# Splitting the operands of a projection into high and low parts, and moving one slab of products into the norms ahead of it

## The chip, the cores and the metric

The kernel runs on one NeuronCore of a Trainium2 chip, in one launch. The metric is device microseconds of an execution: the median of several runs, and beside it one profiled execution, from which every row below comes. The engines are TensorE (PE in rows; PEld its weight loads), VectorE (DVE), ScalarE (ACT), GpSimd (POOL) and the DMA queues, which SyncE (SP) and GpSimd issue. TensorE writes to eight banks of PSUM of 512 fp32 columns each. Its clock has two levels in this trace: 1.0 (2.4 GHz) and 0.50 (1.2 GHz) in the column of the granted clock.

## The reference, cut to what matters

Two transformer blocks follow each other over x of [1024 tokens, 1024]. All arithmetic is fp32. The change touches the end of the first block's mixers and the seam between the two blocks:

```
y  = concatenate([y_a, y_b, y_c, y_d], axis=-1) @ w_out          # [1024, 1024] @ [1024, 1024]
x1 = layer_norm(ALPHA * x + g1 * y, ln1_w, ln1_b)
h  = x1 * (1 + sc2) + sh2
x2 = layer_norm(ALPHA * x1 + g2 * swiglu(h, w_ffn_in, w_ffn_out), ln2_w, ln2_b)
...
h3   = rms_norm(x2, norm_mix_2)
proj = h3 @ w_in_2      # r_q, r_k, r_v, r_g, d_q, d_c, d_pe, d_g, i_q, i_k, i_w
```

The 440 columns d_c, d_pe, i_q, i_k and i_w of `proj` are the first slab of the projections; the others follow in slabs of 512 columns.

## The kernel before, in words

The program is a chain of stages, each a block of its own: all five engines run their own hand-written list of instructions, tied by semaphores, and a stage begins when every engine has ended the last one. Tokens are cut into eight tiles of 128; `i` or `n` names a tile, `k` one of eight groups of 128 features.

**Mixers** (`stage_mixers`, block at L894). In its end VectorE normalises the first mixer's heads in two halves (L1396 to L1406), asking ScalarE for a square root in each (L1204), TensorE transposes them (L1135) and ScalarE drains them into `yT` (L1207). After the last attention product SyncE loads `w_out` in four transfers of two k (L919).

**Join** (`stage_join`, L1409). For each tile TensorE makes `y @ w_out` in fp32 (L1458): two halves of 512 columns, eight k each, every product two instructions. VectorE multiplies by g1 out of PSUM (L1501), adds ALPHA x (L1505), norms (L1522 to L1528), applies sc2 and sh2 (L1510, L1511) into one of two buffers `jn_h`. GpSimd stores x1 (L1437). After the matmuls of tile i TensorE transposes `jn_h` of tile i - 1 (L1448) into banks 4 to 7, ScalarE drains it as the high part (L1470: a copy that rounds to fp32r) and VectorE subtracts it to get the low part (L1489). The two pairs of banks 0, 1 and 2, 3 take the products of even and odd tiles.

**Feed-forward** (`stage_ffn`). All products are made of high and low parts (`product`, L1538): high x high, high x low and low x high, three fp32r matmuls for one product. It takes the tokens in two halves h, and begins with tiles 0 to 3. Per unit of 24 matmuls ScalarE makes the high part of a weight tile (L1643), VectorE the low part (L1729). The hidden layer is a loop of eleven iterations of four units, of which the first stands alone.

**End of the first block** (`stage_first_end`, L1810). Tiles 4 to 7 are transposed back (`back`, L1852), normed on VectorE (`norm`, with L1934 first), scaled on ScalarE by a row sum (`size`, `inverse`, `scale`), weighed on GpSimd (L1835) and, like tiles 0 to 3, transposed (`turn`, L1863), drained by ScalarE (`take`, L1883) and VectorE (`low`, L1947).

**Projections** (`stage_project`). Weights come by k (L2040, four buffers), ScalarE and GpSimd split them (L2133, L2226), and slab 0 runs with k outside and the eight tiles inside, into eight banks. While it runs VectorE makes the angles of the rotary embedding, after positions, frequencies and a gain have been loaded behind the first four weights.

Of the kernel before, what the change touches and what calls it, by code (L numbers as in the profile page):

```python
# [120 lines left out]
def setup(nc, I, out):  # L121
# [23 lines left out]
    K.yT = [at(f"yT{k}", 24 + 4 * k, [P, T]) for k in range(6)] + [K.ydT[:, k, :] for k in range(2)]  # L145
# [667 lines left out]
def stage_mixers(K):  # L813
# [17 lines left out]
    K.wo_in = K.sem("mx_woin")  # L831
# [62 lines left out]
    with nc.Block() as block:  # L894
        @block.sync
        def _(sp):
# [21 lines left out]
            for k in range(0, KT, 2):  # L918
                sp.dma_start(K.wo[:, k:k + 2, :], wo[:, k:k + 2, :]).then_inc(K.wo_in, 16)  # L919
# [220 lines left out]
        def _(act):  # L1140
# [268 lines left out]
def stage_join(K):  # L1409
# [6 lines left out]
    h = [K.at(f"jn_h{s}", 48 + 4 * s, [P, D]) for s in range(2)]  # L1416
# [4 lines left out]
    mm, mev, sq, x1r, hr, tr, thi, tev, chain = (K.sem("jn_" + n) for n in "mm mev sq x1r hr tr thi tev chain".split())  # L1421
    stored = [K.sem(f"jn_st{s}") for s in range(2)]
    with nc.Block() as block:
# [18 lines left out]
        def _(pe):  # L1442
            def turn(i):
# [3 lines left out]
                for k in range(KT):  # L1447
                    last = nc.tensor.transpose(K.bank[4 + 2 * (i % 2) + k // 4][:, (k % 4) * P:(k % 4 + 1) * P],  # L1448
                                               h[i % 2][:, k * P:(k + 1) * P], K.ident[:])
                last.then_inc(tr, 1)  # L1450

            pe.wait_ge(K.wo_in, 16 * KT // 2)
            for i in range(NT):
                if i >= 2:
                    pe.wait_ge(mev, i - 1)
                for b in range(2):
                    for k in range(KT):
                        last = nc.tensor.matmul(K.bank[2 * (i % 2) + b][:], K.yT[k][:, i * P:(i + 1) * P], wo[:, k, b * HALF:(b + 1) * HALF],  # L1458
                                                start=(k == 0), stop=(k == KT - 1))
                last.then_inc(mm, 1)  # L1460
                if i:
                    turn(i - 1)
            turn(NT - 1)

        @block.scalar
        def _(act):
# [5 lines left out]

            for i in range(NT):
                act.wait_ge(sq, 2 * i + 1)
                nc.scalar.activation(rs, rs, ACT.Sqrt).then_inc(sq, 1)
                if i:
                    take(i - 1)
            take(NT - 1)

        @block.vector  # L1480
        def _(dve):
# [9 lines left out]

            dve.wait_ge(r_in, 32)
            dve.wait_ge(K.mod_in, 32)
            for i in range(NT):
# [13 lines left out]
                if i >= 2:  # L1508
                    dve.wait_ge(tr, i - 1)
                link(v.scalar_tensor_tensor(out=h[i % 2][:], in0=K.MOD[:, 4 * D:5 * D], scalar=1.0, in1=y[:], op0=ALU.add, op1=ALU.mult))  # L1510
                v.tensor_tensor(h[i % 2][:], h[i % 2][:], K.MOD[:, 3 * D:4 * D], ALU.add).then_inc(hr, 1)  # L1511
                if i:
                    low(i - 1)
            low(NT - 1)
# [30 lines left out]
def stage_ffn(K):  # L1545
# [33 lines left out]
    def loop(eng, body, count, unrolled=False):  # L1579

        body(0)
        if unrolled:
            for r in range(1, count):
                body(r)
        else:
            with eng.Fori(1, count) as r:
                body(r)
# [10 lines left out]
    with nc.Block() as block:  # L1598
        @block.sync
        def _(sp):  # L1600
            for h in range(2):
# [13 lines left out]
                loop(sp, hidden, NF // FT)  # L1615
# [22 lines left out]
        def _(act):  # L1638
# [21 lines left out]
            for h in range(2):  # L1660
                def hidden(r):
                    for j in range(FT):
# [5 lines left out]
                        elif h:  # L1668
                            take(0, u - 1, KT - 1, 1)
                        if h and j == 0:  # L1670
# [19 lines left out]
                loop(act, hidden, NF // FT, unrolled=(h == 1))  # L1690
# [4 lines left out]
        def _(dve):  # L1695
# [44 lines left out]
            for h in range(2):  # L1740
                def hidden(r):
                    for j in range(FT):
# [3 lines left out]
                        if j or not first(r):  # L1746
                            multiply(h, u - 1, r * FT + (j - 1), 1 - j)
                        if h and j == 0 and r in (3, 5, 7, 9):
# [12 lines left out]
                loop(dve, hidden, NF // FT, unrolled=(h == 1))  # L1761
# [1243 lines left out]
```

## Time and profile before

| | |
|---|---|
| median of 3 runs | 2301.65 us (2300.84 to 2301.83) |
| the profiled execution | 2300.69 us |
| its span, first to last instruction | 2298.9 us |
| TensorE busy | 2140.2 us, 93% |
| VectorE busy | 1257.4 us, 55% |
| ScalarE busy | 717.9 us, 31% |
| GpSimd busy | 402.5 us, 18% |
| mean granted clock | 0.961 |

The shares are means over stages with different limits; what a stage is bound by is read from its own rows. A row of the order of time gives start, duration, engine, line, operation, output <- inputs, and in brackets how long the engine had been idle and what ended that.

### The profile page before, as it was taken

The page shows a single profiled execution, that of the slowest core. Times are in us where ns is not written, and L with a number is a line of the kernel's source. Part 1 is how long each engine was busy: PE and PEld are TensorE (multiplying, and loading weights), DVE is VectorE, ACT ScalarE, POOL GpSimd, SP SyncE. Part 2 cuts the span into 40 slices and gives each one's busy share as a digit, 9 for nine tenths or more (in the row PEclk, how much of TensorE's full clock was granted, in tenths as well). Part 3 has the DMA queues.
Part 4 walks back from the last instruction along what each step waited for, and adds up shares of the span by engine and source line. Part 5 has one row for each costly group of instructions (what it writes and reads, how often), then busy time and mean ns, then how long its engine had stood idle before and what let it go on. Part 6 is the DMA issues. An engine that isn't in the chain of part 4 may idle for free. (4 is left out here: it accounts for less than half of the span.)

```text
span 2298.9 us, 27514 instructions
## 1 busy us (share of the span) xinstructions
PE 2140.2 (93%) x10421; PEld 1576.5 (69%) x10421; DVE 1257.4 (55%) x2203; ACT 717.9 (31%) x1268; POOL 402.5 (18%) x485
## 2 busy tenths in 40 slices
PE   7998999996979999999999998699999878989998
PEld 3744464584438888888888886665888764758876
DVE  6581895286763333223454324358999677762433
ACT  2222021111002323223444223346221335761416
POOL 2900011050000000000000000323656540300210
PEclk8999999997989999999999999799999988999999
DMA  8543110003213333335334232222211002003101
GB/s 313 160 133 115 47 40 1 0 2 119 73 64 112 98 98 89 87 96 160 120 110 128 80 101 68 56 60 56 69 51 46 28 1 82 1 9 130 65 1 73
DMA packets 187509, 180.54 MB, mean 79 GB/s; under 512 B 12982, under 2 KB 157686, under 8 KB 184074
## 3 DMA queue, kind: packets, MB, share of 16 engines
q1 hardware_dynamic: 184426, 168.61, 23.7%
q0 software_dynamic: 2880, 10.49, 1.2%
q8 instruction: 67, 1.10, 0.2%
q14 instruction: 40, 0.33, 0.0%
q10 hardware_dynamic: 96, 0.02, 0.0%
HBM read 165.18 MB, written 12.60 MB: 77 GB/s over the span
## 5 line engine op out<-in xcount | busy, mean ns | idle before, releaser
L1729 DVE TENSOR_TENSOR ff_part<-ff_raw,ff_part 128x1024 fp32r<-128x1024 f32 (+2 forms) x152 | 164.9, 1085 | 434.2 <-ACT ff_part L1643 434.2
L1540 PE MATMUL ps<-h,ff_part 128*128 128x512 f32 x704 | 275.3, 391 | 4.5 <-DVE ff_part L1729 4.5
L1643 ACT ACTIVATE ff_part<-ff_raw 128x1024 fp32r<-128x1024 f32 (+2 forms) x152 | 144.0, 948 | 433.4 <-PE ps L1542 430.6
L1541 PE MATMUL ps<-h,ff_part 128*128 128x512 f32 x704 | 274.8, 390 | 0.0
L1542 PE MATMUL ps<-h,ff_part 128*128 128x512 f32 x704 | 274.6, 390 | 0.0
L1540 PE MATMUL ps<-pj_part,h 128*128 128x512 f32 (+1 forms) x448 | 178.0, 397 | 6.9 <-POOL pj_part L2226 6.7
L1541 PE MATMUL ps<-pj_part,h 128*128 128x512 f32 (+1 forms) x448 | 174.8, 390 | 0.0
L1542 PE MATMUL ps<-pj_part,h 128*128 128x512 f32 (+1 forms) x448 | 174.4, 389 | 0.0
L2284 DVE TENSOR_SCALAR_CACHE_REDUCE pj_junk<-NM,prm 128x384 uint8<-128x384 f32 (+1 forms) x186 | 163.7, 943 | 1.1
L1540 PEld LDWEIGHTS ps<-h,ff_part 128*128 128x128 f32 x704 | 132.7, 188 | 32.4 <-DVE ff_part L1729 4.9
L1542 PEld LDWEIGHTS ps<-h,ff_part 128*128 128x128 f32 x704 | 132.7, 188 | 27.8
L1541 PEld LDWEIGHTS ps<-h,ff_part 128*128 128x128 f32 x704 | 132.7, 189 | 27.3
L1540 PE MATMUL ps<-ff_hid,ff_part 128*128 128x512 f32 x352 | 136.9, 389 | 0.0
L1541 PE MATMUL ps<-ff_hid,ff_part 128*128 128x512 f32 x352 | 136.9, 389 | 0.0
L1542 PE MATMUL ps<-ff_hid,ff_part 128*128 128x512 f32 x352 | 136.9, 389 | 0.0
L2226 POOL TENSOR_TENSOR pj_part<-pj_raw,pj_part 128x512 fp32r<-128x512 f32 (+1 forms) x72 | 93.9, 1308 | 171.4 <-ACT pj_part L2133 170.1
L1540 PEld LDWEIGHTS ps<-pj_part,h 128*128 128x128 f32 x448 | 85.4, 191 | 37.4 <-issue 14.2
L1540 PE MATMUL ps<-w_end,se_hT 128*128 128x512 f32 x256 | 106.9, 418 | 0.4 <-DVE se_hT L2934 0.4
L1000 PE MATMUL ps<-mx_w,HT 128*128 128x272 f32 (+1 forms) x320 | 106.2, 493 | 0.0
L2133 ACT ACTIVATE pj_part<-pj_raw 128x512 fp32r<-128x512 f32 (+1 forms) x72 | 45.4, 632 | 178.3 <-DMA pj_raw<-in_w_in 175.4
L1542 PE MATMUL ps<-w_end,se_hT 128*128 128x512 f32 x256 | 99.9, 390 | 0.0
L1541 PE MATMUL ps<-w_end,se_hT 128*128 128x512 f32 x256 | 99.7, 390 | 0.0
(567 smaller groups left out, 3853.1 us busy)
## 6 DMA issues: line engine op xcount, KB each, us to landing
ff_raw<-in_w_ffn_in SPq DMA_DIRECT2D x88, 512.0 KB, 3.7
s_wm<-in_w_mod SPq DMA_DIRECT2D x16, 1024.0 KB, 4.8
pj_raw<-in_w_in SPq DMA_DIRECT2D x64, 256.0 KB, 2.6
ff_raw<-in_w_ffn_out SPq DMA_DIRECT2D x32, 384.0 KB, 3.2
ff_raw<-in_w_ffn_out SPq DMA_DIRECT2D x32, 320.0 KB, 3.1
mod_w<-in_w_mod SPq DMA_DIRECT2D x8, 1024.0 KB, 8.9
mod_x<-in_x SPq DMA_DIRECT2D x8, 512.0 KB, 14.4
w_out<-in_w_out SPq DMA_DIRECT2D x4, 1024.0 KB, 8.7
```

Of the source, the lines that this page charges most:

```text
L1000: mm = nc.tensor.matmul(bank[:, 0:cols], lhs, rhs, start=(k == 0), stop=(k == KT - 1))
L1540: nc.tensor.matmul(out, w[0], x[0], start=first, stop=False)
L1541: nc.tensor.matmul(out, w[0], x[1], start=False, stop=False)
L1542: return nc.tensor.matmul(out, w[1], x[0], start=False, stop=last)
L1643: nc.scalar.activation(part[s % 2][0][:, 0:n, :], raw[s][:, 0:n, :], ACT.Copy).then_inc(hi, 1)
L1729: v.tensor_tensor(part[s % 2][1][:, 0:n, :], raw[s][:, 0:n, :], part[s % 2][0][:, 0:n, :].bitcast(F32), ALU.subtract).then_inc(lo, 1)
L2133: nc.scalar.activation(part[k % NR][0][:, 0:cols], raw[k % NR][:, 0:cols], ACT.Copy).then_inc(S["hi"], 1)
L2226: g.tensor_tensor(part[k % NR][1][:, 0:cols], raw[k % NR][:, 0:cols], part[k % NR][0][:, 0:cols].bitcast(F32), ALU.subtract).then_inc(S["l ...
L2284: last = v.tensor_scalar(junk[:, packed(j + 2)], x, bound(j), 0.0, ALU.is_ge, ALU.add, accum_out=cnt[:, j:j + 1])
```

## The change

In the **join**, w_out and y are split into high and low parts and multiplied by `product`. ScalarE makes the high parts of w_out: seven inside the mixers, around the two square roots, after waiting for GpSimd's last sum into `mx_H`, and the eighth in the join; VectorE makes the eight low parts at the start of the join, in place. Per tile ScalarE makes the high part of y (`high_y`, 768 and 256 columns), GpSimd the low part (`low_y`). Tile 0 runs in three passes sorted by kind: high x high of all k, then high x low, then low x high; the other tiles run k by k. `jn_h` has four buffers; only tiles 0 to 3 are transposed in the join, tiles 4 to 7 in iterations 1 and 2 of the feed-forward's first hidden loop, whose first three iterations are now written out.

In the **end of the first block** the 440 columns' weights are loaded, split by ScalarE and GpSimd, and the products of tiles 0 to 3 (`mix`) stand on TensorE between the transposes, into banks 4 to 7; the transposes have the pair of banks 2, 3 alone and `back` the pair 0, 1. The norm's last two instructions are a step of their own (`spread`), behind the drains of a tile. In the **projections** only tiles 4 to 7 of slab 0 are left.

The core of the diff:

```diff
@@ stage_mixers @@
+            def wo_split(k):
+                act.wait_ge(K.wo_in[k // 2], 16)
+                nc.scalar.activation(K.wo_high[k][:], K.wo[:, k, :], ACT.Copy).then_inc(K.wo_split, 1)
+
+            act.wait_ge(S["hadd"], 2 * NT)
             for half in range(2):
+                wo_split(2 * half)
+                wo_split(2 * half + 1)
                 act.wait_ge(S["readout"], 2 * half + 1)
...
+            for k in range(4, KT - 1):
+                wo_split(k)
@@ stage_join @@
+            def low_y(i):
+                t = slice(i * P, (i + 1) * P)
+                pool.wait_ge(yhi, 2 * i + 2)
+                nc.gpsimd.tensor_tensor(y6_low[:, :, t], y6[:, :, t], yh[i % 2][:, 0:6, :].bitcast(F32), ALU.subtract).then_inc(ylo, 1)
+                nc.gpsimd.tensor_tensor(yd_low[:, :, t], K.ydT[:, :, t], yh[i % 2][:, 6:, :].bitcast(F32), ALU.subtract).then_inc(ylo, 1)
+
+            low_y(0)
+            low_y(1)
+            for i in range(NT):
+                if i + 2 < NT:
+                    low_y(i + 2)
                 pool.wait_ge(x1r, i + 1)
...
+                if i == 0:
+                    pe.wait_ge(yhi, 2)
+                    for p, (yp, wp) in enumerate(((0, 0), (0, 1), (1, 0))):
+                        if p == 2:
+                            pe.wait_ge(ylo, 2)
+                        for k in range(KT):
+                            if p < 2:
+                                pe.wait_ge((K.wo_split, wl)[p], k + 1)
+                            for b in range(2):
+                                o, y, w = parts(k, b)
+                                last = nc.tensor.matmul(o, y[yp], w[wp], start=(p == 0 and k == 0), stop=(p == 2 and k == KT - 1))
+                else:
+                    pe.wait_ge(ylo, 2 * i + 2)
                     for k in range(KT):
-                        last = nc.tensor.matmul(K.bank[2 * (i % 2) + b][:], K.yT[k][:, i * P:(i + 1) * P], wo[:, k, b * HALF:(b + 1) * HALF],
-                                                start=(k == 0), stop=(k == KT - 1))
+                        for b in range(2):
+                            last = product(nc, *parts(k, b), k == 0, k == KT - 1)
                 last.then_inc(mm, 1)
-                if i:
+                if 1 <= i <= NT // 2:
                     turn(i - 1)
-            turn(NT - 1)
...
+            for k in range(KT):
+                dve.wait_ge(K.wo_in[k // 2], 16)
+                dve.wait_ge(K.wo_split, k + 1)
+                v.tensor_tensor(wo_low[:, k, :], wo[:, k, :], K.wo_high[k][:].bitcast(F32), ALU.subtract).then_inc(wl, 1)
@@ stage_ffn @@
+                        if j == 0:
+                            for i in turned(h, r):
+                                if i >= 6:
+                                    pe.wait_ge(tev, 2 * (i - 5))
+                                for k in range(KT):
+                                    last = nc.tensor.transpose(turn_bank(i, k // 4)[:, (k % 4) * P:(k % 4 + 1) * P],
...
@@ stage_first_end @@
+            def mix(i):
+                pe.wait_ge(tev, 2 * i + 2)
+                for k in range(KT):
+                    if i == 0:
+                        pe.wait_ge(K.pj["lo"], k + 1)
+                    product(nc, K.bank[4 + i][:, 0:N_MIX], [x[:, k, i * P:(i + 1) * P] for x in K.h3], [w[:] for w in K.mixed[k]],
...
             back(2)
+            mix(0)
             turn(4)
             back(3)
-            for i in range(5, NT):
-                turn(i)
+            mix(1)
+            turn(5)
+            mix(2)
+            turn(6)
+            mix(3)
+            turn(7)
...
             norm(0)
             low(0)
+            spread(0)
             low(1)
             inverse(0)
```

TensorE at the start of the join, before: the 16 products of tile 0 read `w_out` itself (the rows give one per k and half).

```order
L894 UNCONDITIONAL_BRANCH
L1441 UNCONDITIONAL_BRANCH
L1458 MATMUL ps<-w_out,yT_52 128x512
L1458 MATMUL ps<-w_out,yT_53 128x512
L1458 MATMUL ps<-w_out,yT_54 128x512
```

The same place in the changed kernel; `w_out_hi` and `w_out_lo` are the parts of w_out, `jn_yh` and `jn_y6l` those of y.

```order
L1498 MATMUL ps<-w_out_hi_1877,jn_yh_4091 128x512 x2
L1498 MATMUL ps<-w_out_hi_1878,jn_yh_4091 128x512 x2
L1498 MATMUL ps<-w_out_lo,jn_yh_4091 128x512 x16
L1498 MATMUL ps<-w_out_hi_1871,jn_y6l 128x512 x2
L1498 MATMUL ps<-w_out_hi_1872,jn_y6l 128x512 x2
```

The 16 products of each kind stand together, and all 16 with `w_out_lo` lie between the other two kinds.

ScalarE in the end of the mixers, before: the last exponential, the table load for the square root, the two roots, the drains.

```order
L1200 ACTIVATE mx_arg_1895<-mx_arg_1895 128x512
L1204 ACT_TABLE_LOAD
L1204 ACTIVATE prm<-prm 128x16 x2
L1207 ACTIVATE yT_52<-ps 128x512
L1207 ACTIVATE yT_53<-ps 128x512
```

The same place in the changed kernel:

```order
L1203 ACTIVATE mx_arg_1898<-mx_arg_1898 128x512
L1206 ACTIVATE w_out_hi_1871<-w_out 128x1024
L1206 ACTIVATE w_out_hi_1872<-w_out 128x1024
L1214 ACT_TABLE_LOAD
L1214 ACTIVATE prm<-prm 128x16
L1206 ACTIVATE w_out_hi_1873<-w_out 128x1024
L1206 ACTIVATE w_out_hi_1874<-w_out 128x1024
L1214 ACTIVATE prm<-prm 128x16
L1206 ACTIVATE w_out_hi_1875<-w_out 128x1024
L1206 ACTIVATE w_out_hi_1876<-w_out 128x1024
L1206 ACTIVATE w_out_hi_1877<-w_out 128x1024
L1219 ACTIVATE y_52<-ps 128x512 x4
```

The table load now stands behind the first two splits, each root has two splits ahead of it, and the four drains have three.

GpSimd in the end of the first block, before: stores of x2 and the weighing of the scaled rows.

```order
L1839 DMA x<-fe_t_8094 128x1024
L1839 DMA x<-fe_t_8095 128x1024
L1835 TENSOR_TENSOR fe_h_8097<-fe_h_8097,fe_rows 128x1024
L1839 DMA x<-fe_t_8096 128x1024
L1835 TENSOR_TENSOR fe_h_8098<-fe_h_8098,fe_rows 128x1024
```

The same place in the changed kernel, from the last two of the eight splits on:

```order
L1933 TENSOR_TENSOR pj_mix_8801<-pj_mixraw_8810,pj_mix_8800 128x440
L1933 TENSOR_TENSOR pj_mix_8803<-pj_mixraw_8811,pj_mix_8802 128x440
L1936 DMA x<-fe_t_8780 128x1024
L1936 DMA x<-fe_t_8781 128x1024
L1929 TENSOR_TENSOR fe_h_8783<-fe_h_8783,fe_rows 128x1024
L1936 DMA x<-fe_t_8782 128x1024
L1929 TENSOR_TENSOR fe_h_8784<-fe_h_8784,fe_rows 128x1024
```

The eight splits stand ahead of all stores and weights.

## Rows read from the trace of the kernel before

**Rows 1.** Order of time, TensorE, the join: start us, duration us, engine, line, count, [idle before]
```profile
552.33 7.21 PE L1458 MATMUL ps<-w_out,yT 128*128 128x512 f32 x12 [0.94 <-PEq L894]
...
567.96 5.31 PE L1458 MATMUL ps<-w_out,yT 128*128 128x512 f32 x12
...
581.69 1.04 PE L1448 MATMUL ps<-ident,jn_h 128*128 128x128 f32 x8
...
669.35 1.04 PE L1448 MATMUL ps<-ident,jn_h 128*128 128x128 f32 x8
```

**Rows 2.** Order of time, VectorE, tile 0 of the join: its first and last instruction
```profile
568.26 1.29 DVE L1501 TENSOR_TENSOR jn_t<-ps,MOD 128x512 f32<-128x512 f32 x2 [18.90 <-PE ps L1458]
...
576.70 1.23 DVE L1511 TENSOR_TENSOR jn_h<-jn_h,MOD 128x1024 f32<-128x1024 f32 x1
```

**Rows 3.** Order of time and DMA issues (the second), the join's end
```profile
676.99 0.53 POOL L1437 DMA_DIRECT2D x<-jn_t  x1 [14.07 <-DVE jn_t L1528]
...
x<-jn_t POOLq DMA_DIRECT2D x1, 512.0 KB, 2.9
...
681.90 1.29 DVE L1489 TENSOR_TENSOR h<-ps,h 128x512 fp32r<-128x512 f32 x2 [1.49 <-ACT h L1470]
...
684.73 0.38 SPq L1606 DMA_DIRECT2D ff_raw<-in_w_ffn_in  x1
```

**Rows 4.** Busy time by stretch: stretch, us, engines, granted clock, DMA share, GB/s
```profile
560.00:680.00 120.00, 111.12 (x303) 52.43 (x302) 82.84 (x110) 8.43 (x22) 4.45 (x8) 0.98 0.18 60
1440.00:1444.00 4.00, 0.78 (x4) 0.79 (x5) 3.57 (x7) 1.36 (x3) 2.96 (x2) 0.50 0.32 131
```

**Rows 5.** Order of time, VectorE, end of the first block: first norm, last norm, last instruction
```profile
1417.51 1.28 DVE L1934 SCALAR_TENSOR_TENSOR fe_t<-fe_x,ps 128x512 f32<-128x512 f32 x2 [7.30 <-PE ps L1852]
...
1441.61 1.28 DVE L1934 SCALAR_TENSOR_TENSOR fe_t<-fe_x,ps 128x512 f32<-128x512 f32 x2
...
1455.76 1.29 DVE L1947 TENSOR_TENSOR h<-ps,h 128x512 fp32r<-128x512 f32 x2 [1.00 <-ACT h L1883]
```

**Rows 6.** Order of time, SyncE and TensorE, opening of the projections and end of slab 0
```profile
1457.31 3.66 SPq L2040 DMA_DIRECT2D pj_raw<-in_w_in  x8
...
1461.80 0.74 PE L1540 MATMUL ps<-pj_part,h 128*128 128x440 f32 x1 [6.71 <-POOL pj_part L2226]
...
1502.82 0.39 PE L1540 MATMUL ps<-pj_part,h 128*128 128x512 f32 x1
```

**Rows 7.** Order of time, TensorE, fp32r matmuls of 512 columns in the feed-forward
```profile
692.19 0.63 PE L1542 MATMUL ps<-h,ff_part 128*128 128x512 f32 x1
692.62 0.63 PE L1540 MATMUL ps<-h,ff_part 128*128 128x512 f32 x1
...
1394.82 0.39 PE L1540 MATMUL ps<-ff_hid,ff_part 128*128 128x512 f32 x1
...
1414.99 0.39 PE L1542 MATMUL ps<-ff_hid,ff_part 128*128 128x512 f32 x1
```

**Rows 8.** Order of time, GpSimd and VectorE, subtractions beside each other
```profile
1432.49 2.36 POOL L1835 TENSOR_TENSOR fe_h<-fe_h,fe_rows 128x1024 f32<-128x1024 f32 x1
...
1525.27 1.28 POOL L2226 TENSOR_TENSOR pj_part<-pj_raw,pj_part 128x512 fp32r<-128x512 f32 x1 [9.44 <-ACT pj_part L2133]
...
1525.38 2.25 DVE L2265 TENSOR_TENSOR MS<-MS,pj_kvr 128x1024 f32<-128x1024 f32 x1
```

**Rows 9.** Loads of w_out (first two), then order of time, ScalarE
```profile
L919 SPq DMA_DIRECT2D w_out<-in_w_out x4: 368/470/651, 530.1 to 531.5; - x4
...
DMA to landing us min/median/max: 4.8/8.7/11.6
...
527.03 1.28 ACT L1204 ACT_TABLE_LOAD   x1
537.95 0.22 ACT L1204 ACTIVATE prm<-prm 128x16 f32<-128x16 f32 x1 [9.64 <-DVE prm L1401]
...
699.25 1.06 ACT L1643 ACTIVATE ff_part<-ff_raw 128x1024 fp32r<-128x1024 f32 x1 [7.35 <-PE ps L1542]
```

More of the change, by code:

```diff
@@ L1901, in _ @@
             root(0)
+            split(0)
+            split(1)
             take(1)
             size(0)
+            for k in range(2, KT):
+                split(k)
             take(2)
@@ L1908, in _ @@
             size(1)
-            for n in range(2, NL):
-                root(n)
-                scale(n - 1)
-                take(n + 2)
-                size(n)
-            scale(NL - 1)
-            take(NT - 2)
-            take(NT - 1)
+            root(2)
+            scale(1)
+            take(4)
+            size(2)
+            root(3)
+            scale(2)
+            take(5)
+            size(3)
+            scale(3)
+            take(6)
+            take(7)
         @block.vector
@@ L1955, in _ @@
             low(2)
+            spread(1)
             low(3)
@@ L1959, in _ @@
             low(4)
+            spread(2)
             inverse(2)
@@ L2041, in load @@
                     at += n
-            for k in range(NR):
-                load(k, k, (C_LAT, M_IQ), (C_IDX, N_IDX))
             with nc.allow_non_contiguous_dma(reason="positions as columns"):
@@ L2048, in _ @@
             sp.dma_start(kvr[:], I["kv_norm_2"].to_broadcast([P, LAT])).then_inc(S["prm"], 16)
-            for k in range(NR, KT):
-                load(k, k, (C_LAT, M_IQ), (C_IDX, N_IDX))
             for half in range(4):
@@ L2061, in _, with mix @@
         def _(pe):
+            def mix(i):
+                for k in range(KT):
+                    last = product(nc, K.bank[i - NH][:, 0:N_MIX], [x[:, k, i * P:(i + 1) * P] for x in K.h3], [w[:] for w in K.mixed[k]],
+                                   k == 0, k == KT - 1)
+                last.then_inc(S["tm"], 1) if i < NT - 1 else last.then_inc(S["um"], KT)
             def slab(j):
-                first = isinstance(j, int) and j == 0
-                cols = N_MIX if first else HALF
                 for k in range(KT):
@@ L2067, in slab @@
                     for i in range(NT):
-                        if k == 0 and not first:
+                        if k == 0:
                             pe.wait_ge(S["ev"], (j - 3) * NT + i + 1)
-                        last = product(nc, K.bank[i][:, 0:cols], [x[:, k, i * P:(i + 1) * P] for x in K.h3], [w[:, 0:cols] for w in part[k % NR]],
-                                       k == 0, k == KT - 1)
+                        last = product(nc, K.bank[i][:], [x[:, k, i * P:(i + 1) * P] for x in K.h3], [w[:] for w in part[k % NR]], k == 0, k == KT - 1)
                         if k == KT - 1 and i < NT - 1:
@@ L2095, in turn @@
                 nc.tensor.transpose(b[:, 2 * P:3 * P], ikd[:, i, :], K.ident[:]).then_inc(S["itr"], 1)
-            slab(0)
+            for i in range(NH, NT):
+                mix(i)
             queries(0, lead - 6)
@@ L2164, in take @@
                     evacuate(j, i, K.bank[i])
-            split(0, range(4))
             act.wait_ge(S["angr"], 1)
@@ L2169, in _ @@
             nc.scalar.activation(cos[:], quar[:], ACT.Sin).then_inc(S["tab"], 1)
-            split(0, range(4, KT))
             split(1, range(3))
```

173 lines of the change are left out of this document (118 added, 55 removed).

## The prediction

> **What bounds the kernel now.** I read the granted clock first, then the instructions of each engine in order of time around the places that the diff touches. The reader is to see three stretches. In the join (552 to 684 us) TensorE is never out of work between tiles: 32 fp32 matmuls take 581.69 - 567.96 = 13.73 us, eight transposes 0.88 more, and tile follows tile to 669.35 [rows 1]. VectorE needs only 577.93 - 568.26 = 9.7 us for a tile's norm, about 11 with the two drains of 1.29 together [rows 2, 3], and waits for TensorE. So TensorE's matmuls bound the join until 669.35; then a tail of 684.73 - 669.35 = 15.4 us follows, in which the last norm, the last transposes, their drain and the block's end come one after another [rows 1, 3]. In the end of the first block (1416 to 1457 us) VectorE bounds: it is busy 3.57 of 4 us where TensorE is busy 0.78, at a granted clock of 0.50 [rows 4], and three rounds of norm take 1441.61 - 1417.51 = 24.1 us [rows 5]. In the first slab of the projections TensorE bounds again: its block opens at 1457.31, the first product waits for loads and splits until 1461.80, and the first 512-column product comes at 1502.82 [rows 6].
>
> **The join's matmuls.** A tile has 16 products (eight k, two halves), each of them two instructions in fp32; each becomes three fp32r matmuls, so 48 stand in place of 32. The same shape stands in the feed-forward: ninety of them in a row start 1414.99 - 1394.82 = 20.17 us apart, 89 gaps of 0.227 us [rows 7]. A tile is 48 x 0.227 = 10.9 us, 2.84 less than 13.73; seven tiles give -19.9 us. A sentence apart: by the Trainium skill (TensorE: Matmul & The Clock Gate, "Wait — 56ns, not 53.3ns?") such matmuls start 215.7 ns apart when the clock is full; eight tiles would then be 4.3 us shorter still; the rows measure 227 and I stay with them. Two of the six transposed tiles that lay between matmuls leave (-1.8), and the transposes of tile 0 now wait some 0.7 for VectorE.
>
> **Tile 0.** It is sorted by kind of product because its parts are not ready: first all y_high x w_high, then x w_low, then y_low. ScalarE opens the join with the split of y (768 + 256 columns; 0.85 + 0.35 as an estimate from its 1.06 for 1024 [rows 9]), so TensorE starts at 553.5, at the low clock level. Then it needs eight w_low from VectorE, 1.23 us each [rows 2], and GpSimd makes y_low for tiles 0 and 1 at the same time. Here the trace speaks against the change: a two-operand VectorE instruction of 1.23 us that meets a GpSimd subtraction of 1.28 takes 2.25 [rows 8]; one of them waits until the other is through. The Trainium skill (SBUF — State Buffer, "Who interferes with whom") calls this an exclusive lock on the shared port pair; by that rule the two engines' times add up whenever VectorE reads two SBUF operands, and the trace agrees. GpSimd's 768 + 256 columns are 1.8 + 0.7 us by its 1.28 for 512 and 2.36 for 1024 [rows 8], 5.1 us for two tiles, of which some 4.4 fall among VectorE's eight: w_low is complete at 552.3 + 9.6 + 4.4 = 566.3, and TensorE ends tile 0 after one more pass, 0.45 + 16 x 0.227 = 4.1 us, at 570.4, against 567.96 before: **+2.4**. Without any meeting it would be 566.0.
>
> In the later tiles GpSimd's y_low starts about 1.4 us after a tile's last product, when VectorE turns to its first instruction with two SBUF operands (1.3 after its start [rows 2]): who comes first is open, and costs VectorE 0.6 to 1.8 us a tile. Its tile is then 11.5 to 12.7 us against TensorE's 11.8, so nearly even; lag is taken up by the two pairs of banks, and I count only the 0.7 above. Last product: 669.35 + 2.4 - 19.9 - 1.8 + 0.7 = 650.8, **-18.6 in all**.
>
> **The join's tail.** Transposes, drain and subtraction of tiles 4 to 7 move to the feed-forward. What is late next is the store of the last tile: issued 676.99 - 669.35 = 7.6 us after the last product, landed 2.9 later, and the block closed 1.5 after its last work, 683.19 to 684.73 [rows 3]. 7.6 + 2.9 + 1.5 = 12.0 in place of 15.4: **-3.4**. VectorE's last instruction (about 9.9) is under that.
>
> **In the feed-forward** 32 transposes join TensorE's stream in iterations 1 and 2: 4 x 0.88 = **+3.5**. Their drains give ScalarE 2.2 and VectorE 2.6 us per iteration, beside units of 24 x 0.227 = 5.4 us in which ScalarE splits for 1.06 and VectorE for 1.23; the cover is about 3 us, and if it is gone each iteration stalls for 1 or 2.
>
> **Before the join** ScalarE makes seven high parts of w_out. The first pair of rows lands 4.8 us after 530.1, so two splits fill 534.9 to 537.0; the table load of 1.28 that stood at 527.03 now comes behind them and ends at 538.3, and the square root that ran at 537.95 waits for it [rows 9]: **+0.35**. The other splits lie beside VectorE's norm or TensorE's transposes.
>
> **End of the first block.** New: four tiles of mix products on TensorE, 16 loads, eight splits on ScalarE, eight on GpSimd (1.1 us each, from 1.28 for 512 columns), one pair of banks instead of two for the transposes, and `spread` behind `low`. The rounds of VectorE lengthen: two SBUF operands in `sub` and `spread` meet GpSimd's nine us of splits (0.7 in round 0, 0.5 + 0.8 in round 1), and `inverse` now waits for ScalarE's row sum, 0.5 to 1.6 us a round, because `spread` comes last before it. Walking the four queues with the durations of rows 5 and 8 gives norm starts 1417.5, 1427.5, 1437.3, 1447.8. The last `spread` ends 1455.7; its store's issue and two weights of 2.36 on GpSimd [rows 8] end at 1461.1. Tile 6 is transposed at 1459, then 24 mix products (4.8 us at the full, 8.8 at the low level, I take 5.9), the eight transposes of tile 7 and their halves drained: 1467.9 against 1457.05, **+10.8**. It is 1466 if all mixing is at full clock, 1478 if none is. Behind the waits for w stand `mix(0)` and then `turn(4)` on TensorE; `turn(4)` waits for GpSimd anyway.
>
> **The slab's rest.** Block opening 0.6 later, 1468.5; four tiles x 24 x 0.200 = 19.2 us follow at once, weights being there. The 200 ns are 440/512 of 227, rounded up. First 512-column product at 1487.7 against 1502.82: with the +10.8 inside, **-15.1**. What runs after it (angles, slab 1) needs about 15 us from the opening and has 19.
>
> **Sum**: -18.6 - 3.4 + 3.5 + 0.35 - 15.1 = -33.3. The profiled execution took 2300.69 us, 0.96 under the median of the runs shown; 2300.7 - 33.3 = 2267.4, and I say **2268** against the median.
>
> **The rivals.**
> 1. *VectorE and GpSimd hardly meet in the join.* For it: the later tiles' meeting is a coin toss, and loads and norms before never stretched. Against it: [rows 8], and eight w_low back to back leave no gap. Tile 0 ends at 566.0, 4.4 us earlier: 2264.
> 2. *Mix products stay at the low level.* The clock was 0.50 in the four us shown of this stretch [rows 4]. The end comes at 1478, and the first half of the next four tiles is slow as well, 2 us: +12, 2280. Against it: TensorE now does more than twice the work there, and continuous work raises it soon: at the join's start the first twelve matmuls took 7.21 us, the same twelve of the next tile 5.31 [rows 1].
> 3. *The feed-forward stalls on the drains*, 2 us twice, and the store lands after 4.9 us as its fellows did rather than 2.9: +6, 2274.
> 4. *Slower.* In the join itself TensorE starves for w_low at 559 to 566 us and is left at the low clock level for the tiles after. There a matmul takes 0.427 (692.19 to 692.62) instead of 0.227 [rows 7]: 336 x 0.2 = +67, so 2335. It decides from 167 of the 336 at the low level. Against it: 120 us at 0.98 before, with TensorE's share of the time about what it will be [rows 4].
> 5. *The change doesn't do what it says*: the three passes of tile 0 gain nothing, since the last w_low is what ends it. That is part of my sum (+2.4).
>
> **How the numbers follow.** Forecast 0.55; rival 1 0.15, rival 2 0.12, rival 3 0.12, rival 4 0.03, small unnamed effects that eat the gain 0.03. The range spans rivals 1 to 2 and the bounds of the walk (1466: -2; join clock at the start: +3): 2260 to 2280. A measurement of this kernel can tell 0.2%, 4.6 us, from no change. Faster 0.95, same 0.02, slower 0.03.
>
> **What would show it.** Right: 48 matmuls per join tile in 10.9 us; tile 0 ending near 570 with VectorE's w_low stretched to 2 or 3 us wherever GpSimd subtracts; the feed-forward's first load near 663; norms of the end 9.5 to 10.5 us apart in place of 8.0; its block closing near 1468; no wait at the projections' opening. Wrong: a granted clock of 0.50 in the join after tile 1, TensorE waiting for `jn_h` or `y_low` in each tile, or the mix products waiting for `pj_mix` after 1440.

## The result, and the profile after

| | before | after |
|---|---|---|
| median of 4 runs | 2301.74 us (2300.84 to 2303.09) | 2269.86 us (2268.64 to 2273.5) |
| ratio, 95% interval | | 0.9867 (0.9853 to 0.988) |
| profiled execution, its span | 2300.69, 2298.9 us | 2270.93, 2269.1 us |

The forecast of 2268 us was 1.9 us under the median, and the time lies inside its range of 2260 to 2280. The sum behind it was 3.5 us too large for the profiled execution: 33.3 us forecast, 2298.9 - 2269.1 = 29.8 measured. I cut both traces at the same events: opening of the join (SyncE's load of the norm's rows), VectorE's first instruction on tile 0 and on tile 7, opening of the feed-forward, first transpose of the end of the first block, first 512-column product of the projections. That gives the terms:

| term | forecast | before, us | after, us | measured |
|---|---|---|---|---|
| span up to the join's opening | +0.35 | 552.27 | 551.24 | -1.0 |
| tile 0 | +2.4 | 15.99 | 20.63 | +4.6 |
| tile 0 to tile 7 | -21.0 | 101.29 | 80.36 | -20.9 |
| tail | -3.4 | 15.18 | 12.78 | -2.4 |
| feed-forward | +3.5 | 731.68 | 735.45 | +3.8 |
| end of block and slab | -15.1 | 86.41 | 73.15 | -13.3 |
| all behind | 0 | 796.1 | 795.5 | -0.6 |

**Tile 0**, TensorE in order of time (start, duration, engine, line, what, count, [idle before]); it answers to the first row of [rows 1]:

```profile
552.48 5.78 PE L1498 MATMUL ps<-w_out_hi,jn_yh 128*128 128x512 f32 x16 [2.12 <-ACT jn_yh L1519]
558.10 1.98 PE L1498 MATMUL ps<-w_out_lo,jn_yh 128*128 128x512 f32 x8
561.01 0.73 PE L1498 MATMUL ps<-w_out_lo,jn_yh 128*128 128x512 f32 x2 [0.93 <-DVE w_out_lo L1548]
562.68 0.75 PE L1498 MATMUL ps<-w_out_lo,jn_yh 128*128 128x512 f32 x2 [0.94 <-DVE w_out_lo L1548]
563.82 2.35 PE L1498 MATMUL ps<-w_out_lo,jn_yh 128*128 128x512 f32 x4 [0.39 <-DVE w_out_lo L1548]
565.97 4.84 PE L1498 MATMUL ps<-w_out_hi,jn_y6l 128*128 128x512 f32 x12
570.65 1.09 PE L1498 MATMUL ps<-w_out_hi,jn_ydl 128*128 128x512 f32 x4
```

The same stretch on VectorE and GpSimd, order of time; it answers to [rows 2] and [rows 8]:

```profile
551.37 13.53 DVE L1548 TENSOR_TENSOR w_out_lo<-w_out,w_out_hi 128x1024 fp32r<-128x1024 f32 x8 [3.03 <-PEq L897]
...
573.20 2.73 DVE L1562 SCALAR_TENSOR_TENSOR jn_t<-jn_x,jn_t 128x1024 f32<-128x1024 f32 x1
...
552.50 2.91 POOL L1455 TENSOR_TENSOR jn_y6l<-y,jn_yh 128x768 fp32r<-128x768 f32 x1 [21.37 <-ACT jn_yh L1519]
555.37 1.72 POOL L1456 TENSOR_TENSOR jn_ydl<-ydT,jn_yh 128x256 fp32r<-128x256 f32 x1
```

The eight subtractions that make the low parts of w_out (w_low below) take 13.53 us, where eight of 1.23 [rows 2] would take 9.8, and TensorE waits three times for one. Then the third pass runs at 0.40 us a matmul, mostly at the low level, where I had put 0.227. Busy time by stretch (us, PE, PEld, DVE, ACT, POOL, granted clock, DMA share, GB/s) shows the clock: it had risen, fell over the waits, and came back in mid-pass. In the tiles after it is at the full:

```profile
556.00:560.00 4.00, 4.00 (x17) 2.96 (x15) 4.00 (x3) 0.00 (x0) 4.00 (x3) 0.94 0.92 372
560.00:564.00 4.00, 1.74 (x6) 0.78 (x6) 4.00 (x4) 0.00 (x0) 1.55 (x1) 0.91 0.01 3
564.00:568.00 4.00, 4.00 (x9) 2.78 (x10) 0.90 (x1) 0.00 (x0) 0.00 (x0) 0.50 0.02 4
568.00:572.00 4.00, 4.00 (x14) 3.16 (x14) 0.13 (x1) 0.23 (x1) 0.00 (x0) 0.74 0.00 0
...
572.00:652.00 80.00, 79.53 (x367) 65.76 (x365) 77.15 (x92) 12.00 (x27) 25.22 (x19) 1.00 0.25 79
```

**The join's end**, order of time, and between its first two rows one of the DMA issues (columns: how many, KB each, us to landing); it answers to [rows 3]:

```profile
652.23 1.29 DVE L1558 TENSOR_TENSOR jn_t<-ps,MOD 128x512 f32<-128x512 f32 x2 [0.90 <-PE ps L1598]
...
659.67 0.53 POOL L1464 DMA_DIRECT2D x<-jn_t  x1 [10.02 <-DVE jn_t L1584]
...
x<-jn_t POOLq DMA_DIRECT2D x1, 512.0 KB, 2.8
...
660.67 1.22 DVE L1568 TENSOR_TENSOR jn_h<-jn_h,MOD 128x1024 f32<-128x1024 f32 x1
...
665.01 7.04 SPq L1671 DMA_DIRECT2D ff_raw<-in_w_ffn_in  x5
```

**End of the first block**, order of time: VectorE's four norms, the wait of the third `inverse`, then ScalarE, GpSimd and TensorE around tiles 6 and 7, and the opening of the projections; it answers to [rows 5] and [rows 6]:

```profile
1401.57 1.29 DVE L2056 SCALAR_TENSOR_TENSOR fe_t<-fe_x,ps 128x512 f32<-128x512 f32 x2 [7.60 <-PE ps L1949]
1410.80 1.28 DVE L2056 SCALAR_TENSOR_TENSOR fe_t<-fe_x,ps 128x512 f32<-128x512 f32 x2
1420.43 1.29 DVE L2056 SCALAR_TENSOR_TENSOR fe_t<-fe_x,ps 128x512 f32<-128x512 f32 x2
1430.27 0.16 DVE L2073 RECIPROCAL prm<-prm 128x1 f32<-128x1 f32 x1 [1.54 <-ACT prm L1591]
1430.46 1.28 DVE L2056 SCALAR_TENSOR_TENSOR fe_t<-fe_x,ps 128x512 f32<-128x512 f32 x2
...
1433.78 1.14 ACT L2013 ACTIVATE fe_h<-fe_t,prm 128x1024 f32<-128x1024 f32 x1
...
1438.47 0.59 POOL L1936 DMA_DIRECT2D x<-fe_t  x1 [6.42 <-DVE fe_t L2069]
1439.09 4.67 POOL L1929 TENSOR_TENSOR fe_h<-fe_h,fe_rows 128x1024 f32<-128x1024 f32 x2
...
1441.50 1.97 PE L1960 MATMUL ps<-ident,fe_h 128*128 128x128 f32 x8 [3.50 <-POOL fe_h L1929]
1443.12 0.72 PE L1596 MATMUL ps<-pj_mix,h 128*128 128x440 f32 x1
1443.64 0.57 PE L1597 MATMUL ps<-pj_mix,h 128*128 128x440 f32 x1
1444.00 0.57 PE L1598 MATMUL ps<-pj_mix,h 128*128 128x440 f32 x1
...
1447.52 0.36 PE L1596 MATMUL ps<-pj_mix,h 128*128 128x440 f32 x1
...
1449.92 1.03 PE L1960 MATMUL ps<-ident,fe_h 128*128 128x128 f32 x8
...
1452.73 0.38 SPq L2180 DMA_DIRECT2D prm<-in_positions  x1
...
1452.79 0.44 PE L1596 MATMUL ps<-pj_mix,h 128*128 128x440 f32 x1 [1.84 <-PEq L1914]
...
1473.61 0.39 PE L1596 MATMUL ps<-pj_part,h 128*128 128x512 f32 x1
```

TensorE stands idle for 3.50 us ahead of tile 6. Behind that, the first products of the fourth mix tile (the slab's 24 products of one of tiles 0 to 3) start 0.37 us apart instead of 0.20. The scaled tile 6 had been ready since 1434.9; GpSimd began to weigh it at 1439.1, because it stands behind the store of tile 7 in GpSimd's list and that waits for the norm of tile 7.

### The profile page after: what moved, and what is told of

It is laid out like the page before. It is cut to its first block and busy times, and to the rows that moved or that the text cites. A ratio compares the mean times of both kernels' runs of the same rounds, so it can differ in the third digit from the quotient of the medians.

```text
span 2269.1 us, 27732 instructions
## 1 busy us (share of the span) xinstructions
PE 2117.0 (93%) x10549; PEld 1599.9 (71%) x10549; DVE 1278.9 (56%) x2211; ACT 733.0 (32%) x1292; POOL 435.1 (19%) x501
## 5 line engine op out<-in xcount | busy, mean ns | idle before, releaser
L1596 PE MATMUL ps<-pj_part,h 128*128 128x512 f32 x384 | 153.2, 399 | 0.2 <-ACT PJ L2273 0.2
L1597 PE MATMUL ps<-pj_part,h 128*128 128x512 f32 x384 | 150.4, 392 | 0.0
L1598 PE MATMUL ps<-pj_part,h 128*128 128x512 f32 x384 | 150.2, 391 | 0.0
L2358 POOL TENSOR_TENSOR pj_part<-pj_raw,pj_part 128x512 fp32r<-128x512 f32 x64 | 84.7, 1326 | 160.3 <-ACT pj_part L2268 159.0
L1596 PEld LDWEIGHTS ps<-pj_part,h 128*128 128x128 f32 x384 | 72.5, 189 | 29.4 <-issue 14.4
L1003 PEld LDWEIGHTS ps<-mx_w,HT 128*128 128x128 f32 x320 | 60.7, 190 | 44.2 <-issue 38.0
```

What stands on the lines that cost most here:

```text
L1003: mm = nc.tensor.matmul(bank[:, 0:cols], lhs, rhs, start=(k == 0), stop=(k == KT - 1))
L1596: nc.tensor.matmul(out, w[0], x[0], start=first, stop=False)
L1597: nc.tensor.matmul(out, w[0], x[1], start=False, stop=False)
L1598: return nc.tensor.matmul(out, w[1], x[0], start=False, stop=last)
L2358: g.tensor_tensor(part[k % NR][1][:], raw[k % NR][:], part[k % NR][0][:].bitcast(F32), ALU.subtract).then_inc(S["lo"], 1)
```

## The experiments

All twelve runs, measured between the same events as above. "Rounds" are the distances between the starts of VectorE's four norms at the end of the first block; "to slab 1" is from that block's first transpose to the first 512-column product. The join is from opening to opening. These sections come from one profiled execution of each kernel.

| kernel | median, us | ratio (95%) | tile 0 | join | rounds | to slab 1 |
|---|---|---|---|---|---|---|
| before | 2301.74 | | 15.99 | 132.46 | 8.26, 8.25, 7.59 | 86.41 |
| the change | 2269.86 | 0.9867 (0.9853 to 0.988) | 20.63 | 113.77 | 9.23, 9.63, 10.03 | 73.15 |
| join_only | 2284.67 | 0.9936 (0.9919 to 0.9952) | 18.84 | 111.98 | 8.26, 8.24, 7.59 | 86.73 |
| end_only | 2285.72 | 0.9934 (0.9915 to 0.9952) | 16.79 | 133.25 | 9.24, 9.65, 10.55 | 70.87 |
| t0_kbyk | 2271.90 | 0.988 (0.9864 to 0.9897) | 20.08 | 113.21 | 9.23, 9.63, 9.99 | 73.11 |
| no_meeting | 2264.24 | 0.9853 (0.9835 to 0.9872) | 14.65 | 107.77 | 9.13, 9.63, 10.63 | 70.87 |
| mix3_split | 2265.75 | 0.9847 (0.983 to 0.9863) | 20.56 | 113.70 | 9.23, 9.65, 9.75 | 65.69 |
| mixes_out_late | 2290.31 | 0.9954 (0.9937 to 0.9971) | 18.89 | 112.07 | 8.98, 9.23, 9.44 | 91.20 |
| spread_in_norm | 2269.21 | 0.9859 (0.9842 to 0.9875) | 18.91 | 112.07 | 11.16, 11.56, 7.66 | 70.17 |
| combo | 2258.31 | 0.9819 (0.9802 to 0.9835) | 14.60 | 107.77 | 9.23, 9.64, 9.93 | 65.88 |
| weigh_first | 2264.82 | 0.9845 (0.9828 to 0.9861) | 18.84 | 111.98 | 9.13, 9.64, 10.32 | 67.37 |
| hybrid | 2262.23 | 0.983 (0.9814 to 0.9847) | 14.60 | 107.77 | 9.13, 9.64, 9.73 | 67.87 |
| change_again | 2271.35 | 0.9862 (0.9846 to 0.9877) | 20.61 | 113.78 | 9.24, 9.63, 10.01 | 73.12 |
| meet_and_weigh | 2261.29 | 0.9818 (0.9805 to 0.9831) | 14.63 | 107.77 | 9.14, 9.63, 10.61 | 67.67 |

The ratios are what to compare between groups of runs; their intervals are 3 to 4 us wide each way. The sections of the trace resolve finer differences: the change and its repetition agree within 0.06 us in each.

### The two halves apart

`join_only` is the change with the last two stages as they were before; `end_only` is the kernel before with those two stages of the change.

> The join, its splits and the moved transposes alone; the end of the first block and the projections as before. My theory (two independent gains): opening of the join to opening of the feed-forward 113.8 us instead of 132.5, +0.3 before it, +3.8 in the feed-forward: about -14.6, 2287 us. Rival (the two halves share something, such as a clock that is granted less elsewhere when the join is denser): this half brings 18 or more alone, and the two halves together less than their sum by over 3 us.

> The moved slab alone; the join as before. My theory: end of the first block 11.4 us longer, the projections up to the first 512-column product 24.7 shorter, net -13.3, so about 2288 us, and 73 us from the first block's end's first transpose to the first 512-column product instead of 86.4. Rival: with the join's gain gone this half brings another amount (over 16 or under 10).

The halves save 0.64% and 0.66%, together 1.30% against the change's 1.33%: they add up as far as the intervals tell, which leave some 6 us open. By the medians neither sign of the rival came: `join_only` brings some 15 us, under its 18, and `end_only` some 15, between 10 and 16. Without the moved transposes the feed-forward takes 732.0 us (`end_only`), with them 736.1 (`join_only`); in the other kernels that have them it is 734.9 to 736.7. Two sections differ from the change's by other than its parts: in `join_only` tile 0 takes 18.84 instead of 20.63, though not one instruction of it differs, and in `end_only` the slab comes after 70.87 instead of 73.15. In `join_only` the third pass of tile 0, in the order of time, and the stretch around its start (columns as above) are

```profile
566.40 3.07 PE L1498 MATMUL ps<-w_out_hi,jn_y6l 128*128 128x512 f32 x12
...
564.00:568.00 4.00, 3.91 (x12) 2.67 (x12) 1.32 (x2) 0.00 (x0) 0.00 (x0) 0.66 0.01 4
```

The clock fell over the waits here too, but it was back at the full almost as this pass began; the change took 4.84 us for it. Of the seven profiled executions with this tile 0, three took 20.6 us (the change, its repetition, `mix3_split`) and four 18.8 to 18.9. So the same instructions met the low clock in that pass, and 1.8 us with it, in some and not in others. What decides it is open: the only kernel profiled twice, the change, took 20.6 both times.

The opening of the projections shows the same. From there to the first 512-column product, with the same instructions, seven of the eleven profiled executions took 20.9 us and four (`end_only`, `no_meeting`, `mix3_split`, `combo`) 19.3. These 1.5 us are in the last column of the table and belong to none of the edits as far as the runs show.

### Tile 0: sorting, and the meeting

`t0_kbyk` does not sort tile 0:

```diff
-                    for p, (yp, wp) in enumerate(((0, 0), (0, 1), (1, 0))):
...
+                    pe.wait_ge(ylo, 2)
+                    for k in range(KT):
+                        pe.wait_ge(wl, k + 1)
+                        for b in range(2):
+                            last = product(nc, *parts(k, b), k == 0, k == KT - 1)
```

> Tile 0 of the join k by k like the others, with a wait for each w_low. [...] Theory B (sorting matters because TensorE would otherwise start late at the low clock): 48 x 0.427 = 20.5 us from there, tile 0 ends 26 us after the opening, total +6.

TensorE starts at 557.84 instead of 552.5, and tile 0 takes 20.08 us. The clock makes up for part of the late start: the products come dense, it rises at 564, and stays up. The first product in the order of time, and the stretches:

```profile
557.84 0.77 PE L1592 MATMUL ps<-w_out_hi,jn_yh 128*128 128x512 f32 x1 [6.80 <-POOL jn_ydl L1456]
...
560.00:564.00 4.00, 4.00 (x11) 3.07 (x11) 4.00 (x3) 0.00 (x0) 2.17 (x2) 0.51 0.05 20
564.00:568.00 4.00, 4.00 (x19) 3.29 (x18) 1.52 (x2) 0.00 (x0) 0.00 (x0) 1.00 0.02 4
```

The 26 us of theory B did not come. Against the sorted tile 0 with the low clock in its third pass (20.6) the sort brings nothing, against the one without (18.84) it brings 1.2 us. And it is not the last w_low that ends the unsorted tile: once started, TensorE has no wait in it, with 14 gaps of 0.43 us and then 0.23. It is bound by its late start, behind GpSimd's y_low, and the low clock after it. `no_meeting` takes GpSimd out of VectorE's way:

```diff
 GpSimd
-            low_y(0)
+            pool.wait_ge(ylo, 2)
             low_y(1)
 VectorE, behind the eight w_low
+            dve.wait_ge(yhi, 2)
+            v.tensor_tensor(y6_low[:, :, 0:P], y6[:, :, 0:P], yh[0][:, 0:6, :].bitcast(F32), ALU.subtract).then_inc(ylo, 1)
+            v.tensor_tensor(yd_low[:, :, 0:P], K.ydT[:, :, 0:P], yh[0][:, 6:, :].bitcast(F32), ALU.subtract).then_inc(ylo, 1)
```

> y_low of tile 0 on VectorE behind the eight w_low, y_low of tile 1 on GpSimd only after them: GpSimd and VectorE do not meet in tile 0. Theory A (the shared port stretched w_low): VectorE's eight take 9.9 us instead of 13.5, the third pass starts 11.4 us after the opening instead of 14.7; tile 0 ends 17.8 after it if its third pass stays at the low clock (0.40 a matmul), 15.0 if at the full; total -2.7 to -5.5 against the change, about 2266. Theory B (w_low is stretched by something else, loads or ScalarE): still 13.5 us, and total +1 for the added y_low.

Its order of time, VectorE, GpSimd and TensorE in tile 0:

```profile
551.27 9.17 DVE L1548 TENSOR_TENSOR w_out_lo<-w_out,w_out_hi 128x1024 fp32r<-128x1024 f32 x8 [3.03 <-PEq L897]
...
561.72 1.85 POOL L1455 TENSOR_TENSOR jn_y6l<-y,jn_yh 128x768 fp32r<-128x768 f32 x1 [30.75 <-DVE jn_ydl L1551]
563.53 0.74 POOL L1456 TENSOR_TENSOR jn_ydl<-ydT,jn_yh 128x256 fp32r<-128x256 f32 x1
...
557.93 3.79 PE L1498 MATMUL ps<-w_out_lo,jn_yh 128*128 128x512 f32 x16
561.70 3.06 PE L1498 MATMUL ps<-w_out_hi,jn_y6l 128*128 128x512 f32 x12
```

The eight w_low shrink from 13.53 to 9.17 us; the 4.36 is what the prediction had put down for the meeting (4.4). TensorE has no wait between the passes, the clock stays at the full from 557.9 on, and tile 0 ends 6.0 us sooner. Since a tile 0 with the meeting takes 18.84 where the third pass finds the full clock, about 4.2 of the 6.0 are the meeting itself and 1.8 the low clock in that pass. Theory A holds. GpSimd pays as well: its 256 columns take 1.72 us in the meeting and 0.74 alone.

### The fourth mix tile, and GpSimd's order

`mix3_split` puts five of the eight k of `mix(3)` ahead of `turn(6)`:

```diff
+            mix(3, range(5))
             turn(6)
-            mix(3)
+            mix(3, range(5, KT))
             turn(7)
```

> Five of the eight k of the fourth mix tile ahead of the transposes of tile 6, three behind them; all else as the change. Theory A (TensorE's idle 3.5 us ahead of tile 6 cost twice: as time, and by the clock that fell to 0.50 for the 24 products behind it): 15 products fill the idle time, 9 stand between the transposes at the full clock; the block's last work ends 47.5 to 48.5 us after its first transpose instead of 52.0, the slab's rest starts at the full clock; total 4 to 6 us under the change, about 2265. Theory B (the chain through GpSimd's weights and the drains sets the end, the mixing was beside it): block end as before within 1 us.

Tile 7 is transposed 43.55 us after the block's first transpose instead of 49.46, the block's last drain ends at 46.1 (52.0), and the slab's rest starts at the full clock: 65.69 against 73.15. Of these 7.5 us, 5.9 lie ahead of the projections' opening and 1.5 in the clock behind it. The expectation of 47.5 to 48.5 was too cautious, its cause is right. `weigh_first` leaves TensorE's list alone and takes the cause away:

```diff
             for n in range(NL):
+                if n:
+                    weigh(n - 1)
                 pool.wait_ge(x2r, n + 1)
                 pool.dma_start(K.x2[(4 + n) * P:(5 + n) * P, :], t[n % 3][:]).then_inc(stored[n % 3], 16)
-                if n:
-                    weigh(n - 1)
```

> The change, but GpSimd weighs tile n - 1 before it waits for the norm of tile n and stores it. Theory A (the weight of tile 6 was ready to start at 34.5 us after the block's first transpose and stood behind the store of tile 7 until 38.6): tile 6 is transposed at about 37.2 instead of 41.0, right behind the third mix tile, the fourth runs at the full clock, tile 7 is transposed at 42.9 instead of 49.5, and the total is 5 to 7 us under the change, about 2264. Theory B (the scaled tile itself comes late): transposes of tile 6 stay within 1 us of 41.0 and the total within 1.5 us.

Order of time, GpSimd and TensorE:

```profile
1435.68 2.38 POOL L1929 TENSOR_TENSOR fe_h<-fe_h,fe_rows 128x1024 f32<-128x1024 f32 x1 [5.38 <-ACT fe_h L2013]
1439.44 0.59 POOL L1938 DMA_DIRECT2D x<-fe_t  x1 [1.38 <-DVE fe_t L2069]
...
1438.11 1.09 PE L1960 MATMUL ps<-ident,fe_h 128*128 128x128 f32 x8 [0.34 <-POOL fe_h L1929]
```

Tile 6 is transposed at 37.17 us after the block's start instead of 41.04, with 0.34 us of idle time instead of 3.50, and all of `mix(3)` runs at 0.20 a matmul. One moved instruction gives 5.8 us in this section, all of it ahead of the projections' opening (46.5 us after the first transpose instead of 52.3).

### The rounds of the norm

`mixes_out_late` makes all eight tiles of slab 0 in the projections and puts GpSimd's splits behind its last weight. `spread_in_norm` deletes the four calls of `spread` and runs its two instructions at the end of `norm`.

> All eight tiles of the slab's products in the projections, and GpSimd's eight splits behind its last weight: VectorE never meets a split in its norms. Theory A (meeting GpSimd lengthens the rounds of the norm by 0.7 to 1.1 us each, waiting for the row sum by the rest): rounds of 8.5, 8.5 and 9.6 us instead of 9.2, 9.6 and 10.0. Theory B (the order of the steps and the one pair of banks lengthen them): rounds unchanged within 0.3. In both the total is 15 to 20 us over the change, for 96 products more stand bare in the projections.

> The norm's last step back inside the norm, ahead of the drains of a tile. Theory A (the later place takes the wait for the root away but makes one for the row sum, about even): rounds within 0.7 us of the change's, total within 1.5 us of it. Theory B (the later place is what made inverse wait 0.4 to 1.5 us a round): rounds 0.5 to 1.5 us shorter, total -3.

Neither theory on the meeting is right as put. Without it the rounds shrink by 0.25, 0.40 and 0.59 us, 1.2 in all, while they are 4.8 longer than before. The other 3.6 lie in what this run leaves as in the change. `inverse` still waits 0.62, 0.67 and 1.54 us for the row sum, where before it waited 0, 0 and 0.34, and in the third round `low` waits 0.67 for ScalarE where it waited for nothing: together 3.2 us more. The order of the steps and the single pair of banks changed together, and no run separates the two. But putting `spread` back is no cure: the first two rounds become 1.9 us longer each, because the drains of a tile now start later and TensorE and ScalarE deliver the next one later (a wait of 1.24 us in `low`), and only the last, which has one tile to drain instead of two, falls to 7.66. In this run TensorE's gap ahead of tile 6 is 0.18 us:

```profile
1440.71 1.09 PE L1960 MATMUL ps<-ident,fe_h 128*128 128x128 f32 x8 [0.18 <-POOL fe_h L1929]
```

Tile 6 comes no sooner for it (40.7 us after the first transpose, 41.0 in the change; GpSimd's store of tile 7 only 0.3 sooner). TensorE's mix products come 3.0 us later and so fill the gap, and the clock holds through the fourth; that is why the longer rounds cost this section nothing. The median is the change's all the same, and of the profiled execution a part of that lies behind the section: from the first 512-column product to the end it took 798.3 us, `end_only` 798.2, all others 795.0 to 796.4.

`hybrid` takes the late `spread` for two tiles, the early one for the others, with `no_meeting` and `weigh_first`:

> No meeting in tile 0, the weights ahead of the stores, and the norm's last step back inside the norm for the last two tiles only. Expected: rounds of 9.2, 9.6 and 7.7 us (the first two as in the change, the third as in the run with the step in every norm); TensorE then has no gap over 1 us from its first mix product on and is what bounds the block: tile 7 transposed 42.7 to 43.0 us after the first transpose; total 11 to 13 us under the change, 2256 to 2259. If the rounds of the norm still bound the end: the step's place brings 2 us more than that.

The third round is 9.73, not 7.7, tile 7 is transposed at 44.2 us instead of 42.7 to 43.0, and the ratio of 0.983 is some 8.5 us under the change, not 11 to 13. The row of that `spread`, and GpSimd's at the same time (`hybrid`, order of time):

```profile
1422.58 3.40 DVE L2074 SCALAR_TENSOR_TENSOR fe_t<-fe_t,prm,fe_rows 128x1024 f32<-128x1024 f32 x1
...
1422.52 2.37 POOL L1932 TENSOR_TENSOR fe_h<-fe_h,fe_rows 128x1024 f32<-128x1024 f32 x1 [1.83 <-ACT fe_h L2016]
```

The weight that now comes early starts 0.06 us ahead of the `spread` that comes early too, and 1.28 us become 3.40, nearly the 2.37 + 1.28 - 0.06 = 3.59 of one behind the other. In `weigh_first` and in `spread_in_norm` the same `spread` took 1.28: only the two moves together put it beside the weight. By the Trainium skill (SBUF — State Buffer, "Who interferes with whom") one of the two engines is locked out; these rows agree.

### Both causes away

`combo` is `no_meeting` and `mix3_split`; `meet_and_weigh` is `no_meeting` and `weigh_first`, run beside the change itself.

> The kernel without the meeting in tile 0 and with the split fourth mix tile. If the two causes are independent: 6 us from the join and 4 to 6 from the end of the first block, about 2260. If the clock only moved the loss on: not under 2263.

> The change itself once more, beside the last kernel on the same chip: 2267 to 2272 us, join from opening to the feed-forward's opening 113.8 us within 1.5, slab from the first transpose to the first 512-column product 73.1 us, or 70.9 if the clock rises 5 us earlier in the fourth mix tile as it did in two of the other runs.

> The two smallest mends together: no meeting of VectorE and GpSimd in tile 0, and the weights ahead of the stores, with the fourth mix tile whole and in its place. If the two are independent: join 107.8 us from opening to opening, tile 7 transposed 43.6 us after the first transpose, 46.5 to the slab's rest, together 10.5 to 12 us under the change on the same chip, 2257 to 2260. If the loss at the end only wandered between join and slab: less than 8 under it.

Both come out at a ratio of 0.982 to before, and on one chip `meet_and_weigh` is 10.1 us under the change, by its sections 6.0 in the join and 5.5 in the slab, less 1.1 in the feed-forward. That is just under the 10.5 that I expected at the least. The fourth mix tile ran at the full clock, but the clock then fell over the opening of the projections: the slab's rest took 20.9 us in it, 19.3 in `combo`, with the same instructions. To the opening of the projections the two take as long (46.8 and 46.6 us). `hybrid` differs from `meet_and_weigh` in the place of `spread` alone and gains nothing by it (0.983 and 0.9818, 67.87 and 67.67 us). `combo` and `meet_and_weigh` are the best versions of the study; between them the runs do not decide.

## Why the prediction was right, and where it was off

**The matmuls of the join** are the gain, as said. From tile 0 to tile 7 the sum was -19.9 - 1.8 + 0.7 = -21.0 and the traces give -20.9. The 0.227 us from [rows 7] held, at a clock of 1.00. Rival 4, the low clock in the whole join, didn't happen.

**Tile 0** was mis-sized: +2.4 put, +4.6 measured. The stretched w_low were right in mechanism and in price (complete 13.7 us after the opening; 9.6 + 4.4 = 14.0 put). What failed is the step "one more pass, 0.45 + 16 x 0.227 = 4.1 us": the products of the last w_low took 1.1 and the pass 5.8, together 6.9, for waits of TensorE that the pace of w_low brings also brought the clock down. Without the low clock in the third pass tile 0 takes 18.84, still 0.4 more than the 18.4 put. Rival 1, without meeting, was worth 4.4 us in my working, and `no_meeting` measured 6.0. Rival 5 is half right: the last w_low and a pass end the sorted tile 0, but the unsorted one ends as late for another reason, its late start.

**The meeting in later tiles** was left as a coin toss. It happens in every tile in which GpSimd still subtracts, tiles 0 to 5 (`jn_t` 2.2 to 2.8 us instead of 1.22), and costs nothing there, because VectorE still keeps up: of 80 us it is busy 77.15 with the stretches in them, and TensorE 79.53.

**The tail** is 12.8 us from VectorE's start on tile 7, where 15.2 - 3.4 = 11.8 was put. The store was issued when expected (7.4 us after the last norm began) and landed in 2.8; the step that failed is "the block closed 1.5 after its last work". From the landing it took 665.01 - 662.5 = 2.5. The trace says why: behind its wait for the store GpSimd has a DRAIN of 0.71 us (662.75 to 663.46), and the 1.5 begin only then, at 663.50. Before, the same DRAIN (680.12 to 680.82) lay under VectorE's last work.

**The feed-forward** is +3.8 in the change and 4.1 between `join_only` and `end_only`, +3.5 put. The drains stayed hidden; rival 3 falls.

**The end of the first block** came within 0.5 us: its last drain ends 52.0 us after its first transpose, 51.5 put, and the projections open at 52.3, 52.1 put. Rounds of 9.2 to 10.0 were put at 9.5 to 10.5. The walk even held the cause of the largest loss (the two weights behind the last store), but I took it as given and priced the mixing behind it at 5.9 us; it took 7.0. Rival 2 is thus true for about half of one mix tile of four.

**The slab's rest** took 20.9 from opening to the first 512-column product, 19.2 put: the clock was at 0.68 once more from 1455 to 1459. This is the difference between -15.1 and -13.3. In `end_only` and `no_meeting` the clock fell over the same wait of 3.50 us but was back sooner (the fourth mix tile took 5.7 us) and stayed up over the projections' opening; they gave 70.87 us and so -15.5. That the forecast of this term lies between the two is in part luck.

**Before the join** the +0.35 is there, hidden by scatter. VectorE's wait for the first square root grew from 0.28 to 0.60 us, by 0.32 (order of time, before and after):

```profile
538.20 0.25 DVE L1403 RECIPROCAL prm<-prm 128x16 f32<-128x16 f32 x1 [0.28 <-ACT prm L1204]
...
537.17 0.25 DVE L1415 RECIPROCAL prm<-prm 128x16 f32<-128x16 f32 x1 [0.60 <-ACT prm L1214]
```

From the load of w_out to the opening it is 22.2 us before and 22.5 after, but that load was issued 1.3 us earlier.

In short, each mechanism of the sum was there. The terms missed 5.3 us of gain (2.2, 1.0, 0.3 and 1.8), of which some 3.5 are the granted clock after a short wait of TensorE: I had applied it at the join's start and not behind the later waits. An opening of the join 1.0 us earlier, where 0.35 later was put, and 0.6 less at the end gave part of it back; over the kernels here that opening lies between 551.2 and 553.8, so this is scatter, and so is a part of the closeness of 2268 to 2269.86.

## What to carry to other kernels

Once a forecast has TensorE waiting for a few us, price the work behind the wait at the low clock for some of its length, or better, fill the wait with work that is ready: here 3.5 us of waiting cost 2.2 more in the slow products behind it, and 0.9 in two other kernels with the same instructions. When a step is moved to GpSimd to relieve VectorE, look at which instruction of VectorE stands beside it; beside eight subtractions back to back it cost 4.4 us here. And look through the list of a helper engine for a wait that work behind it doesn't need: the weight behind a store was worth 5.8 us for one moved line.

## What the runs showed of the hardware

- The same instructions of a stage do not always meet the same clock: one pass of 12 matmuls took about 3.1 us in four profiled executions and 4.8 in three, and the projections' opening 19.3 us in four and 20.9 in seven. Whether that goes by the execution or by the kernel around it is not shown.
- A GpSimd subtraction of 256 columns takes 0.74 us alone and 1.72 beside VectorE's instructions of 1.23, 768 columns 1.85 alone and 2.91; VectorE's 1.28 became 3.40 behind a GpSimd product of 2.37. The instruction that grows can be of either engine.
- What the end of a stage costs is read from that stage. The join closed 1.5 us after VectorE's last instruction before [rows 3], and 2.5 us after the landing of a store in the change, 0.71 of it GpSimd's DRAIN behind its wait. The end of the first block closed 0.26 us after its last instruction (1457.05 to 1457.31 [rows 5, rows 6]); the join has a clearing of its semaphores in between (0.72 us, 683.71 to 684.43), this block has none.
